# Expert stage of a two-layer trunk: the last tile's rows return to their tokens as products with 0/1 matrices

## The reference, cut to what matters

```python
glog = (x @ w_rg); gsel = argmax(glog)                    # one of 4 groups for each token
top_p, top_i = top_k(softmax(elog of that group), 2)      # two of its 4 experts
gate = one_hot(gsel*4 + top_i) * (gw * top_p/sum(top_p))
hid = silu(x @ w_g[e]) * (x @ w_u[e])                     # 16 experts of width 256
y = sum_e (hid * gate[e]) @ w_d[e]
x = x + g2 * y
```

## Time and profile before

| | |
|---|---|
| time, median of 3 runs | 1861.41 us (1861.28, 1861.41, 1865.58) |
| profiled execution, its own time | 1865.8 us |
| span of its trace | 1864.1 us |
| PE busy | 1682.6 us, 90% |
| DVE busy | 1015.6 us, 54% |
| ACT busy | 874.6 us, 47% |
| POOL busy | 665.6 us, 36% |
| mean granted TensorE clock | 0.961 |

### The profile page before, as it was taken

How to read it: one execution, slowest core, us unless ns; L and a number is a source line. 1 busy time by engine, 2 the same in 40 slices (tenths; PEclk the granted TensorE clock), 3 DMA queues, 4 the chain that set the end, 5 groups by cost and what they waited for, 6 DMA issues and landing times. The chain is left out here.

```text
span 1864.1 us, 30976 instructions
## 1 busy us (share of the span) xinstructions
PE 1682.6 (90%) x10077; PEld 1347.0 (72%) x10077; DVE 1015.6 (54%) x1808; ACT 874.6 (47%) x1495; POOL 665.6 (36%) x425
## 2 busy tenths in 40 slices
PE   2799998999999989999939999989999998899993
PEld 2588786776778767777727878767768787777773
DVE  0215437755452148999850272575644602799995
ACT  1343333444343336878723333434444333478773
POOL 2354354333446641000034544423334666101001
PEclk8899999999999999999959999989999999999997
DMA  9432243333546649999733222433435555799993
GB/s 333 169 102 91 82 141 100 104 133 108 182 147 240 236 140 375 380 383 365 292 132 107 92 98 87 139 97 97 154 136 192 191 195 203 257 408 366 373 364 115
DMA packets 119342, 368.49 MB, mean 198 GB/s; under 512 B 11996, under 2 KB 32028, under 8 KB 119200
## 3 DMA queue, kind: packets, MB, share of 16 engines
q1 hardware_dynamic: 94960, 328.62, 48.5%
q0 software_dynamic: 5760, 21.02, 3.0%
q10 hardware_dynamic: 18480, 17.08, 2.9%
HBM read 345.90 MB, written 20.77 MB: 197 GB/s over the span
## 5 line engine op out<-in xcount | busy, mean ns | idle before, releaser
L724 POOL TENSOR_TENSOR wlo<-raw,whi 128x1024 fp32r<-128x1024 f32 x204 | 491.3, 2415 | 627.0 <-ACT whi L876 626.7
L1220 PE MATMUL G<-whi,hhi 128*128 128x512 f32 (+1 forms) x1440 | 581.6, 404 | 19.1 <-ACT pB L965 8.9
L1222 PE MATMUL G<-whi,hlo 128*128 128x512 f32 (+1 forms) x1440 | 562.5, 391 | 0.0
L1221 PE MATMUL G<-wlo,hhi 128*128 128x512 f32 (+1 forms) x1440 | 562.5, 391 | 0.0
L1220 PEld LDWEIGHTS G<-whi,hhi 128*128 128x128 f32 x1440 | 274.2, 190 | 94.9 <-DVE wlo L1653 17.4
L1222 PEld LDWEIGHTS G<-whi,hlo 128*128 128x128 f32 x1440 | 273.9, 190 | 58.8
L1221 PEld LDWEIGHTS G<-wlo,hhi 128*128 128x128 f32 x1440 | 274.7, 191 | 49.2
L876 ACT ACTIVATE whi<-raw 128x1024 fp32r<-128x1024 f32 x204 | 213.8, 1055 | 183.5 <-PE G L1222 93.9
L1653 DVE TENSOR_TENSOR wlo<-raw,whi 128x1024 fp32r<-128x1024 f32 x144 | 172.4, 1219 | 5.2 <-ACT whi L884 3.4
L884 ACT ACTIVATE whi<-raw 128x1024 fp32r<-128x1024 f32 x144 | 152.7, 1061 | 28.6 <-PE G L1222 18.1
L1653 DVE TENSOR_TENSOR wlo<-pA,whi 128x1024 fp32r<-128x1024 f32 x72 | 87.7, 1223 | 19.6 <-ACT whi L884 17.3
(11 more groups left out here) (319 smaller groups left out, 2482.0 us busy)
## 6 DMA issues: line engine op xcount, KB each, us to landing
raw<-in_units SPq DMA_DIRECT2D x430, 512.0 KB, 5.2
pA<-in_units SPq DMA_DIRECT2D x72, 512.0 KB
pB<-in_units SPq DMA_DIRECT2D x72, 512.0 KB, 6.4
kT<-in_units SPq DMA_DIRECT2D x12, 512.0 KB, 5.6
spare<-in_units SPq DMA_DIRECT2D x12, 512.0 KB, 8.1
y_sorted<-yo POOLq DMA_DIRECT2D x12, 512.0 KB, 6.8
hs<-h_sorted POOLq DMA_DIRECT2D x10, 514.0 KB, 7.4
bias<-in_nat_bias ACTq DMA_DIRECT2D x16, 256.0 KB, 3.1
```

The lines of the kernel that those rows point to most:

```text
L724: lo_done.of(nc.gpsimd.tensor_tensor(wlo[:, k, :], raw[:, POS_OF[g] % RAW, :], whi[:, k, :].bitcast(F32), ALU.subtract))
L1220: nc.tensor.matmul(dst, st_hi, mv_hi, start=start, stop=False)
L1221: nc.tensor.matmul(dst, st_hi, mv_lo, start=False, stop=False)
L1222: return nc.tensor.matmul(dst, st_lo, mv_hi, start=False, stop=stop)
```

## The change

The last tile's result isn't written to HBM. Instead the rows of the last tile go from `yo` to their tokens on PE: for each block t of 128 tokens, a 128x128 matrix `selT` of zeros and ones, which has a one where a token's slot is that row of the last tile, is multiplied with `yo`. The parts are:

- `route`: one more DVE instruction (`slot` less 640), and after `gidx` three that build the 0/1 matrices `sel` by a comparison with 1 to 128.
- In the last tile, after unit 8, PE transposes the three matrices into the bank `O`, and ACT copies them to `selT`.
- POOL issues the three fetches as soon as DVE is through with unit 14 of the last tile, no longer after the last tile's rows have landed. They read the other five tiles' rows; the last tile's place in `y_sorted` is filled with zeros once, by a seventh transfer before the first layer.
- ACT copies `S` to `yo` in two halves.
- PE makes six products of 128x512 (`back_to_tokens`), and for block 1 adds the fetched rows by two more with the identity matrix. These are plain 32-bit products, not split ones.
- DVE adds the products of blocks 0 and 2 to the fetched rows in halves, then goes on as before; for block 1 it reads the sum out of PSUM.
- POOL waits for the last product before it goes into the next layer.

```diff
@@ -72,6 +72,7 @@
+LAST_SEL = 8

@@ -331,6 +332,7 @@
+        selT = prob[:, 1, 1, :]

@@ -353,6 +355,10 @@
         T = ctx.enter_context(nc.psum_tensor("T", [P, 2, 512], F32))
         O = ctx.enter_context(nc.psum_tensor("O", [P, 512], F32))
 
+
+        def last_bank(t, hf):
+
+            return ((G[:, 0, :], G[:, 1, :]), (G[:, 2, :], T[:, 1, :]), (T[:, 0, :], O[:, :]))[t][hf]
 
         w_in = [sg(f"w_in{i}", 16) for i in range(RAW)]
         w_more = [sg(f"w_more{i}", 16) for i in range(RING - RAW)]
...
@@ -538,6 +545,7 @@
             own(tt(cum, cum, at.unsqueeze(1).to_broadcast([P, TILES, GRP]), ALU.add))
             own(tt(cum, cum, gsel, ALU.mult))
             own(V.tensor_reduce(slot, cum, AX, ALU.add))
+            own(V.tensor_scalar(rw[:, :, 13:14], slot, float(-(NT - 1) * P), None, ALU.add))
             slot_dve.of(V.tensor_scalar(slot_at[:, :].unsqueeze(2), slot, -1.0, None, ALU.add))
             need(sg_pe, 0)
             q_gate.of(V.tensor_copy(gate[:, :], O[:, 0:GRP]))
@@ -549,6 +557,10 @@
             for k in range(UT // RAW):
                 gidx_dve.of(V.tensor_scalar(gidx[:, :].rearrange("p (t k) -> p t k", t=OVER)[:, :, k:k + 1],
                                             first.unsqueeze(2), float(RAW * k), None, ALU.add))
+
+            for t in range(TILES):
+                ins = V.tensor_scalar(sel[:, t, :], order[:, 4 + NT:4 + NT + P], rw[:, t, 13:14], None, ALU.is_equal)
+            last_sel.of(ins)
 
         block = ctx.enter_context(nc.Block())
 
@@ -702,6 +714,7 @@
             pool.wait_ge(nx_pe.handle, NEXT)
             for i in range(NT):
                 pool.dma_start(h_sorted[i * P:(i + 1) * P, :], zeros).then_inc(zero_out, 16)
+            pool.dma_start(y_sorted[(NT - 1) * P:NT * P, :], zeros[:, 0:D]).then_inc(zero_out, 16)
             with pool.Fori(0, DEPTH) as l:
                 chain = [0]
 
...
@@ -829,14 +842,15 @@
                         pool.wait_ge(*e_hid.in_tile(l, NT - 2, GRP, GRP - 1))
                         gates(NT - 1)
                         rows_out(NT - 2)
-                        rows_out(NT - 1)
                         hs_in.n += NT - 3
                         y_out.n += NT - 3
-                        pool.wait_ge(*yo_free.in_tile(l, NT - 1, 1, 0))
-                        carry()
+                        pool.wait_ge(*e_lo.in_tile(l, NT - 1, UT, RING + TILES - 1))
+                        carry(14)
                         for t in range(TILES):
                             y_in[t].of(nc.gpsimd.indirect_dma_start(
                                 yacc[:, t, :], None, y_sorted, bass.IndirectOffsetOnAxis(ap=slot_at[:, t:t + 1], axis=0)))
+                        need(last_pe, TILES - 1)
+                        yo_free.of(nc.gpsimd.tensor_tensor(dummy[:, 12:13], ones[:, 0:1], ones[:, 0:1], ALU.mult))
 
 
             pool.wait_ge(fin_sq_act, TILES)
...
@@ -1149,12 +1163,19 @@
                                 if n - 3 == TURN_NEXT and not last:
                                     rows_high(0, i + 1)
                                     rows_high(1, i + 1)
+                                if n - 3 == LAST_SEL and last:
+                                    need(last_selT, 0)
+                                    last_act.of(nc.scalar.activation(selT, O[:, 0:384], ACT.Copy))
                             if not last:
                                 for n in range(UT, UT + 3):
                                     high(i, n)
                             act.wait_ge(*e_unit.in_tile(l, i, UT, UT - 1))
                             act.wait_ge(*yo_free.in_tile(l, i, 1, -1))
-                            yo_act.of(nc.scalar.activation(yo[:, :].rearrange("p (h n) -> p h n", h=2), S[:, :, :], ACT.Copy))
+                            if last:
+                                last_act.of(nc.scalar.activation(yo[:, 0:512], S[:, 0, :], ACT.Copy))
+                                yo_act.of(nc.scalar.activation(yo[:, 512:D], S[:, 1, :], ACT.Copy))
+                            else:
+                                yo_act.of(nc.scalar.activation(yo[:, :].rearrange("p (h n) -> p h n", h=2), S[:, :, :], ACT.Copy))
 
                         with act.Fori(0, NT - 1) as i:
                             one_tile(i, False)
@@ -1591,6 +1612,11 @@
                                     turn_hid(i, TURN_HID.index(n))
                                 if n == TURN_NEXT and not last:
                                     turn(i + 1)
+                                if n == LAST_SEL and last:
+                                    need(last_sel, 0)
+                                    for t in range(TILES):
+                                        mm = nc.tensor.transpose(O[:, t * P:(t + 1) * P], sel[:, t, :], ident[:, :])
+                                    last_selT.of(mm)
 
                         free("T1", "S0", "S1", "O")
                         need(*evacuated(CHUNK_NO["wout", 1], 2))
@@ -1611,6 +1637,23 @@
                         with pe.Fori(0, NT - 1) as i:
                             one_tile(i, False)
                         one_tile(NT - 1, True)
+
+                        def back_to_tokens(t, hf, **flags):
+                            return nc.tensor.matmul(last_bank(t, hf), selT[:, t * P:(t + 1) * P], yo[:, hf * 512:(hf + 1) * 512],
+                                                    **flags)
+
+                        need(last_act, 0)
+                        need(y_in[1], 0)
+                        nc.tensor.matmul(last_bank(1, 0), ident[:, :], yacc[:, 1, 0:512], start=True, stop=False)
+                        need(last_act, 1)
+                        back_to_tokens(0, 0, start=True, stop=True)
+                        pe.wait_ge(*yo_act.in_tile(l, NT - 1, 1, 0))
+                        last_pe.of(back_to_tokens(0, 1, start=True, stop=True))
+                        nc.tensor.matmul(last_bank(1, 1), ident[:, :], yacc[:, 1, 512:D], start=True, stop=False)
+                        back_to_tokens(1, 0, start=False, stop=True)
+                        last_pe.of(back_to_tokens(1, 1, start=False, stop=True))
+                        back_to_tokens(2, 0, start=True, stop=True)
+                        last_pe.of(back_to_tokens(2, 1, start=True, stop=True))
 
 
         @block.vector
@@ -1995,8 +2038,16 @@
                         dve.wait_ge(*g_in.at(l, 3))
                         dve.wait_ge(*m_out.at(l, 5))
                         for t in range(TILES):
+                            halves = [slice(hf * 512, (hf + 1) * 512) for hf in range(2)]
                             dve.wait_ge(*y_in[t].at(l, 0))
-                            own(tt(yacc[:, t, :], yacc[:, t, :], gbc[:, t // 2, :], ALU.mult))
+                            need(last_pe, t)
+                            if t == 1:
+                                own(*(tt(yacc[:, t, h], last_bank(t, hf), gbc[:, t // 2, h], ALU.mult)
+                                      for hf, h in enumerate(halves)))
+                            else:
+                                own(*(tt(yacc[:, t, h], yacc[:, t, h], last_bank(t, hf), ALU.add)
+                                      for hf, h in enumerate(halves)))
+                                own(tt(yacc[:, t, :], yacc[:, t, :], gbc[:, t // 2, :], ALU.mult))
                             ins = tt(x[:, t, :], x[:, t, :], yacc[:, t, :], ALU.add)
                             if t < TILES - 1:
                                 own(ins)
```

More of the change, by code:

```diff
@@ L407, in program @@
         sel_dve, gates_dve, sg_pe = sg("sel_dve"), sg("gates_dve"), sg("sg_pe")
+        last_sel, last_selT, last_act, last_pe = sg("last_sel"), sg("last_selT"), sg("last_act"), sg("last_pe")
         layer_end = sg("layer_end", credit=1)
@@ L796, in _ @@
                     elif s == ("route",):
-                        pool.wait_ge(zero_out, 16 * NT)
+                        pool.wait_ge(zero_out, 16 * (NT + 1))
                         pool.wait_ge(*nb_act.at(l, KD - 1))
@@ L1047, in _ @@
                         else:
-                            act.wait_ge(zero_out, 16 * NT)
+                            act.wait_ge(zero_out, 16 * (NT + 1))
                         nc.scalar.activation(nrow[0:1, d, :], S[0:1, 0, :], ACT.Copy)
```

## The result

The changed kernel takes 1854.18 us (median of 6 runs, 1851.03 to 1858.61), the kernel before 1864.88 (6 runs, 1861.28 to 1868.01). The ratio is 0.9946, 95% interval 0.9927 to 0.9964, which of 1864.88 is 10.1 us less, 6.7 to 13.6; the medians themselves are 10.7 apart. Forecast were 1854.1 us and 7.3 us less. The time was met better than the difference: three runs of the kernel before put its median at 1861.41, six and more at 1864.2 to 1864.9, and the gain is larger than the sum by about as much.

What follows compares the result with a forecast made beforehand. Tiles were taken as bound by PE, layer ends by the path from copy to norm. Terms -3.7 - 6.4 + 2x1.0 + 2x0.37 + 0.1 = -7.3 us, from the median 1861.41, gave 1854.1 us; 8-in-10 range 1849.5 to 1858.8.

Steps and rivals of the forecast that it cites:

- The end of the second layer: Copy to `yo` until the norm, second layer: 13.13 us in place of 16.83, -3.7 us, DVE being the path.
- The end of the first layer: Copy to norm, first layer: 16.95 us in place of 23.34, -6.4 us, with 3.85 for DVE standing beside POOL.
- POOL doesn't hold DVE: Rival, 12%: DVE's addition gets between POOL's or takes turns; first layer's end up to 3.85 shorter, 1850.3 us.
- the upper-bound rival: Rival, 18%: costs at upper bounds, seventh write delays parameters by 1.4, POOL holds the halves too, 0.7; 1856.1 us.
- Route: In `route`, four added DVE instructions delay the tiles' first low part, not given back: +1.0 us per layer.
- The transposes: Last tile: three transposes on PE add +0.37 us per layer, bounds 0.3 and 0.5.
- The seventh write: Before the first layer: 512 KB more of zeros, moving when the parameters are in, 0.1 us; other bound 1.4.
- The sum: Whole kernel: both layer ends, `route`, transposes and seventh write together give -7.3 us.
- The base: Kernel before: median 1861.41 us, from which the forecast of 1854.1 us was taken.
- The rival of the upper level: Rival, 13%: the changed kernel's median falls on the upper of two time levels, 4.3 us higher, 1858.4 us.
- the one of PE out of step: Rival, 5%: in the last tile PE waits 0.58 us for each of 15 units, 8.7 us per layer; 1871.5 us.

Runs made afterwards that it cites:

- x6_fetch_late: Changed kernel, but POOL issues the three fetches only when ACT has made the last `yo`; 1875.55 us, ratio 1.0062 to the kernel before.
- x2_pool_late: Changed kernel, but POOL makes the next layer's two low parts only behind DVE's end of the layer; 1853.5 us, ratio 0.9936 to the kernel before.
- x5_pool_halves: Changed kernel, but POOL makes each of its first two low parts in two instructions of 512 columns; 1849.86 us, ratio 0.9931 to the kernel before.
- x1_build_alone: Kernel before plus only the four DVE instructions in `route` that build the 0/1 matrices, result unread; ratio 1.0013 to the kernel before.
- x4_zero_alone: Kernel before plus only the seventh write of zeros; ratio 1.000 to the kernel before.
- x11_zero_later: Kernel before, but POOL issues its six writes of zeros only after ACT's first square for the norm; ratio 0.9989 to the kernel before.

## Why the prediction was right, and where it was not

**The end of the second layer** held to 0.1 us in each step: PE's products at 0.86 and clock 1.00, DVE's start, then DVE alone as the path, 13.12 us. x6_fetch_late shows what bears it: without the early fetch that end takes 11 us longer, 24.07, which is 7.2 more than before the change.

**The end of the first layer**: 16.69 for 16.95. POOL's work beside it (x2_pool_late: 13.11 without) costs 3.6 where I had 3.85. The size was near by luck, the mechanism half right. I took from one row that DVE stands until POOL has nothing left. That was a right reading of the row (POOL's second part took its usual 2.34 at 943.15), but a wrong rule to carry over: the row is the one meeting of its kind in which POOL went first. Two things came out otherwise. POOL started 2.8 us later than I set it (a pause of 2.76 us between its dummy and its first part, whose cause no run shows), so it met block 2's operations and not block 1's; and DVE gets in between its two parts and waits twice. The Trainium skill, "SBUF — State Buffer", section "SBUF: two separate sides", states an exclusive lock for a whole instruction, not a split of bandwidth. The trace and x5_pool_halves agree: DVE ends 1.08 to 1.09 us behind the end of POOL's instruction, also when that is half as long (1.08 in both meetings). The rival "POOL doesn't hold DVE" is refuted; so is the part of the upper-bound rival that has POOL hold the halves (0.68 us beside POOL in x6_fetch_late).

**Route** was mis-sized: 0.77 us per layer, not 1.0. The three 128x128 instructions delay the low part by 0.59 (712.91 to 713.50), since the next instruction starts before the record of the last ends at 713.73; I had put 0.8 of their 0.86. That nothing gives it back was right (x1_build_alone).

**The transposes** were mis-sized: 0.37 per layer forecast, under 0.1 shown. The step that failed is that I added PE's time for them to the tile in full, with nothing given back, because PE is busy for 33.12 of its 33.59 us. PE's timeline around them, after and before:

```profile
906.55 0.39 PE L1243 MATMUL S<-whi,elo 128*128 128x512 f32 x1
906.78 0.49 PE L1618 MATMUL O<-ident,prob 128*128 128x128 f32 x3
907.02 0.49 PE L1241 MATMUL S<-whi,ehi 128*128 128x512 f32 x1
907.35 0.39 PE L1242 MATMUL S<-wlo,ehi 128*128 128x512 f32 x1
...
908.28 0.39 PE L1243 MATMUL S<-whi,elo 128*128 128x512 f32 x1
908.50 0.47 PE L1241 MATMUL G<-whi,hhi 128*128 128x512 f32 x1
```

```profile
908.08 0.39 PE L1222 MATMUL S<-whi,elo 128*128 128x512 f32 x1
908.61 0.50 PE L1220 MATMUL G<-whi,hhi 128*128 128x512 f32 x1
```

They do cost 0.34 where they stand (0.24 for three, and a step of 0.33 in place of 0.23 behind). But 1.7 us behind them the kernel before had a wait of PE, a step of 0.53 at 908.08 where others are 0.23; it is 0.22 now. That wait pays for nearly all of it. Work put ahead of such a wait of PE is paid by it; the delay in `route` is not, where DVE itself, for whose low part PE waits, is late.

**The seventh write** costs nothing that x4_zero_alone can show; forecast was 0.1, with 1.4 as a rival.

**The sum.** With what was measured it is -6.65 - 3.71 + 2 x 0.20 + 0.60 + 0.55 = -8.8 us, 1.5 more gain than forecast, inside both intervals of the ratio. The profiled executions differ by 12.5. The other 3.7 lie in two stretches where the change does next to nothing. 2.8 of them are in norm to `slot_at` of layer 2, whose value after, 663.06, lies within the spread of the kernel before (662.5 to 665.7); nothing shows that it is more than chance. 0.9 are at the start, and there something is behind it: in seven of nine profiles of the changed kernel and its variants POOL issued its zeros at 36.3 to 37.0 us, behind the last parameter, and the parameters landed at 46.2 to 50.2; in all four of the kernel before and its variants that leave the six writes alone, they were issued at 34.6 to 35.1 and the parameters landed at 51.4 to 52.2. What makes the zeros late is PE, whose products they wait for. In windows from 32 to 36 us (columns as above; first before, then after) PE had clock 1.00 and was through before the zeros' issue at 34.6, or clock 0.50 and was busy until past 36:

```profile
32.00:34.00 2.00, 1.82 (x64) 1.55 (x60) 0.00 (x0) 0.03 (x1) 0.00 (x0) 1.00 0.90 295
34.00:36.00 2.00, 0.44 (x2) 0.20 (x2) 0.19 (x1) 1.44 (x3) 1.39 (x3) 1.00 0.98 326
```

```profile
32.00:34.00 2.00, 1.43 (x28) 1.34 (x32) 0.00 (x0) 0.00 (x0) 0.00 (x0) 0.50 0.81 293
34.00:36.00 2.00, 2.00 (x44) 1.62 (x36) 0.00 (x0) 0.00 (x0) 0.00 (x0) 0.50 0.87 301
```

In these two profiles the zeros are 2.4 us apart; 0.7 of it is that the products start later (32.57 for 31.87), the rest is the clock. So a lower clock there makes the zeros later, and with them late the parameters come earlier: start to `slot_at` is 707.8 to 713.9 in the nine, mean 710.0, against 711.4 to 712.9 in the four. x11_zero_later shows that late zeros and early parameters go together in the kernel before too, so they don't need the changed kernel. In that profile the clock had fallen at 32.8 as well, so it doesn't show what the edit alone brings; the time does, 0.1% and not clear of nothing. That the clock fell there in seven profiles of nine and, without the edit, in none of four may be chance or may not be; it stays open.

**The base** was the largest miss. I read four times of the kernel before as two levels 4.3 us apart. Of the 69 executions of it that were timed beside the other kernels, 67 fill 1856.6 to 1869.3 without a gap over 1 us and two lie above, at 1871.1 and 1874.7; the medians are 1864.2 to 1864.9. My 1854.1 stands on a base 3.5 low and a gain 3.4 low, which cancel: that the time was met to 0.1 us is luck. The rival of the upper level has no ground; neither has the one of PE out of step, since the last tile takes 34.66 and 34.54 us after, 34.59 and 34.54 before the change.

## What to carry to other kernels

When the end of a stage is a round trip through memory, fetch early what is known and keep the last piece on chip; the matmuls that do it should follow the last ones without a gap: after 8.16 us without work they came at half clock. Between DVE and POOL, ask of each pair of instructions that may meet whether DVE reads its tensors from SBUF: it then loses up to one whole POOL instruction, and in one meeting here two, so small POOL instructions, or POOL work beside a DVE instruction that reads PSUM, cost less than one large one (3.6 against 1.45 us here). And where times spread by half a per cent, add up stretches between the same two instructions of several profiles: those of the tiles repeat within 0.2 us, where the interval of six runs against six is 7 us wide.

## What the runs showed of the hardware that I had not expected

- DVE and POOL held each other by whole instructions. DVE went ahead of POOL's next in some dozen meetings of each profile; at the kernel before's layer end POOL went ahead, in all five profiles. The hold applied to DVE's 128x1024 TENSOR_SCALAR with one tensor from SBUF (two in 3.51 us, not 1.42) and to one of 128x16 (2.26, not 0.17), not to one with a PSUM operand: in x6_fetch_late the half at 948.21 has its usual 0.68 though POOL began at 948.15.
- After 8.16 us without work PE's first products of 128x512 in 32 bits took 1.7 us each, at clock 0.50, and 0.86 without the gap.
- With the first write of 3 MB of zeros issued at 38.9 in place of 34.6 us, the parameters, issued on another queue at 33.9 to 35.3 (34.4 to 35.4 before), were there 6.6 us earlier.
